# A hybrid decoder block with 64 experts: gate and up weights issued ahead of the preceding expert's down weights

## The reference

```python
t = h.reshape(B * S, D)
scores = jax.nn.sigmoid((t @ w_router).astype(jnp.float32))
...
w = w / jnp.sum(w, axis=-1, keepdims=True) * ROUTED_SCALE
combine = (jax.nn.one_hot(eidx, N_EXPERTS, dtype=jnp.float32) * w[..., None]).sum(1).astype(t.dtype)
y = (jax.nn.silu(t @ w_sh_gate) * (t @ w_sh_up)) @ w_sh_down
for g in range(N_GROUPS):
    sl = slice(g * EXPERTS_PER_GROUP, (g + 1) * EXPERTS_PER_GROUP)
    a = jax.nn.silu(jnp.einsum('td,edf->tef', t, w_gate[sl])) * jnp.einsum('td,edf->tef', t, w_up[sl])
    y = y + jnp.einsum('tef,efd->td', a * combine[:, sl, None], w_down[sl])
```

## Time and profile before

| | us |
|---|---|
| median of 3 runs | 1158.05 (1157.08 to 1160.28) |
| span of the profiled execution | 1155.5 |
| TensorE busy in it | 1109.0 |
| VectorE, ScalarE, GpSimd busy | 854.7, 783.1, 413.2 |
| q1 (SyncE's queue): moved, share of the 16 engines' time | 254.13 MB, 56.6% |

### The profile page before, as it was taken

The page is one execution under the profiler, slowest core; times in us unless marked ns, Lnnn a source line. Parts: engine busy times, 40 slices in busy tenths (PEclk is TensorE's granted clock), DMA queues, the critical chain, the costliest instruction groups (busy, mean ns, idle before and its releaser), DMA issues. The chain is left out here.

```text
span 1155.5 us, 17715 instructions
## 1 busy us (share of the span) xinstructions
PE 1109.0 (96%) x5459; PEld 909.9 (79%) x5459; DVE 854.7 (74%) x1211; ACT 783.1 (68%) x1266; POOL 413.2 (36%) x477
## 2 busy tenths in 40 slices
PE   7999999999899999999999999999999999999898
PEld 7888888788678886888888887777878878777677
DVE  3536534277664586999999988888899989899665
ACT  6644434367553335888888888788888888887562
POOL 1220000033473002455555553444555555454320
PEclk9999999999999999999999999999999999999999
DMA  6422322113203098999999999999999999999631
GB/s 241 146 73 82 136 73 75 38 60 101 100 2 128 37 367 311 379 322 358 383 388 385 384 386 377 362 359 361 369 362 371 366 365 379 366 369 364 173 123 73
DMA packets 71955, 291.61 MB, mean 252 GB/s; under 512 B 15139, under 2 KB 20550, under 8 KB 46950
## 3 DMA queue, kind: packets, MB, share of 16 engines
q1 hardware_dynamic: 52496, 254.13, 56.6%
q0 software_dynamic: 18768, 34.79, 11.9%
q10 hardware_dynamic: 646, 2.12, 0.5%
HBM read 284.61 MB, written 42.07 MB: 283 GB/s over the span
## 5 line engine op out<-in xcount | busy, mean ns | idle before, releaser
L1518 DVE TENSOR_TENSOR arena_r<-arena,win_r 128x1024 fp32r<-128x1024 f32 x252 | 292.1, 1220 | 51.7 <-ACT win_r L986 46.7
L986 ACT ACTIVATE win_r<-arena 128x1024 fp32r<-128x1024 f32 x252 | 246.2, 1056 | 57.8 <-DMA arena<-in_w_exp_up 53.4
L1929 PE MATMUL bank<-win_r,work_r 128*128 128x512 f32 x512 | 205.3, 401 | 19.6 <-DVE x_low_r L1477 19.1
L669 POOL DMA_INDIRECT moe_sum<-ya,sidx x64 | 121.0, 1890 | 252.4 <-ACT ya L1019 252.4
L1930 PE MATMUL bank<-win_r,x_low_r 128*128 128x512 f32 x512 | 199.4, 390 | 0.0
L1931 PE MATMUL bank<-arena_r,work_r 128*128 128x512 f32 x504 | 197.0, 391 | 0.0
L1492 DVE TENSOR_TENSOR arena_r<-arena,hT_r 128x1024 fp32r<-128x1024 f32 x128 | 150.5, 1218 | 0.0
L1929 PEld LDWEIGHTS bank<-win_r,work_r 128*128 128x128 f32 x512 | 96.3, 188 | 43.8 <-issue 25.9
L1663 PE MATMUL bank<-arena_r,hT_r 128*128 128x512 f32 (+2 forms) x320 | 121.8, 381 | 1.2 <-DVE win_r L1129 1.2
L1667 PE MATMUL bank<-win_r,hT_r 128*128 128x512 f32 (+2 forms) x320 | 120.4, 376 | 0.0
L1664 PE MATMUL bank<-arena_r 128*128 128x512 f32 (+2 forms) x320 | 120.4, 376 | 0.0
(11 more groups left out here) (290 smaller groups left out, 2173.3 us busy)
## 6 DMA issues: line engine op xcount, KB each, us to landing
arena<-in_w_exp_down SPq DMA_DIRECT2D x64, 1024.0 KB, 15.8
arena<-in_w_exp_gate SPq DMA_DIRECT2D x63, 1024.0 KB
arena<-in_w_exp_up SPq DMA_DIRECT2D x63, 1024.0 KB
win<-in_w_in SPq DMA_DIRECT2D x8, 2048.0 KB, 7.7
win<-in_w_o SPq DMA_DIRECT2D x2, 2048.0 KB, 7.9
arena<-in_w_ple_gate SPq DMA_DIRECT2D x2, 2048.0 KB, 24.5
arena<-moe_sum SPq DMA_DIRECT2D x8, 512.0 KB, 7.6
win<-in_mla_w_qb SPq DMA_DIRECT2D x4, 576.0 KB, 4.0
```

Source lines behind the costliest of these rows:

```text
L669: pool.indirect_dma_start(sums[j % 2], bass.IndirectOffsetOnAxis(sidx[j % 2][0:NS, 0:1], 0), yo[j % 2][0:NS], None, bounds_check=last_toke ...
L986: act.activation(gu_hi[n % 2][:, :, cols], raw[:, :, cols], ACT.Copy).then_inc(gu_hi_r, 1)
L1518: dve.tensor_tensor(low_[:, :, cols], raw[:, :, cols], gu_hi[n % 2][:, :, cols].bitcast(F32), ALU.subtract).then_inc(gu_lo_r, 1)
L1929: pe.matmul(b_, x_hi[:, k, :], w_hi, start=(k == 0), stop=False)
```

## The change

SyncE's order of issue. Gate and up of expert e are issued as soon as the slot's gate and up part is free, and the down weights of expert e-1 after them, where before down of e-1 came first. The condition for each transfer is the same as before. The last expert's down weights follow by themselves after the loop. Ahead of the loop, gate and up of expert 8 are issued before down of expert 3 and before the last of the four blocks of the shared result; a wait for expert 4's gate and up to have landed is added there, since both count on the same semaphore.

```diff
             expert_gu(3, 3)
-            for t, (y_, n) in enumerate(((sh_y_act, 1), (sh_y_dve, 1), (sh_y_dve, 2), (sh_y_act, 2))):
-                if t == NT - 1:
-                    sp.wait_ge(sh_dn, NT)
-                    expert_dn(3, 3)
+            def shared_rows(t, y_, n):
                 sp.wait_ge(y_, n)
                 sp.dma_start(sums[1][t * P:(t + 1) * P, :], y_sh[t]).then_inc(sum_odd_st[t // 2], 16)
 
-            for e in range(RING, 3 * RING):
-                sp.wait_ge(gu_done, e - RING + 1)
+            for t, (y_, n) in enumerate(((sh_y_act, 1), (sh_y_dve, 1), (sh_y_dve, 2))):
+                shared_rows(t, y_, n)
+            sp.wait_ge(gu_done, 1)
+            sp.wait_ge(w_gu[0], 64)
+            expert_gu(2 * RING, 0)
+            sp.wait_ge(sh_dn, NT)
+            expert_dn(RING - 1, RING - 1)
+            shared_rows(NT - 1, sh_y_act, 2)
+
+            for e in range(RING + 1, 3 * RING):
                 if e != 2 * RING:
-                    expert_gu(2 * RING if e == EXTRA else e, e % RING)
-                sp.wait_ge(dn_done, e - RING + 1)
-                expert_dn(e, e % RING)
+                    sp.wait_ge(gu_done, e - RING + 1)
+                    expert_gu(e, e % RING)
+                sp.wait_ge(dn_done, e - RING)
+                expert_dn(e - 1, (e - 1) % RING)
             with sp.Fori(3, E // RING) as q:
                 for r in range(RING):
                     sp.wait_ge(gu_done, q * RING + (r - RING + 1))
                     expert_gu(q * RING + r, r, one=False)
-                    sp.wait_ge(dn_done, q * RING + (r - RING + 1))
-                    expert_dn(q * RING + r, r, one=False)
+                    sp.wait_ge(dn_done, q * RING + (r - RING))
+                    expert_dn(q * RING + (r - 1), (r - 1) % RING, one=False)
+            sp.wait_ge(dn_done, E - RING)
+            expert_dn(E - 1, RING - 1)
             sp.wait_ge(nb_ready, 1)
```

More of the change, by code:

```diff
@@ L487, in _ @@
                         expert_gu(e, e % RING)
-                        sp.wait_ge(dn_done, b * E + (e - RING + 1))
-                        expert_dn(e, e % RING)
+                        if e >= 1:
+                            sp.wait_ge(dn_done, b * E + (e - RING))
+                            expert_dn(e - 1, (e - 1) % RING)
                     with sp.Fori(2, E // RING) as q:
@@ L493, in _ @@
                             expert_gu(q * RING + r, r, one=False)
-                            sp.wait_ge(dn_done, b * E + q * RING + (r - RING + 1))
-                            expert_dn(q * RING + r, r, one=False)
+                            sp.wait_ge(dn_done, b * E + q * RING + (r - RING))
+                            expert_dn(q * RING + (r - 1), (r - 1) % RING, one=False)
+                    sp.wait_ge(dn_done, b * E + (E - RING))
+                    expert_dn(E - 1, RING - 1)
             sp.dma_start(pbuf, a["p"][0, 0].rearrange("(t q) n -> q t n", q=P)).then_inc(ld_p, 16)
```

## The result

The changed kernel takes 1164.1 us (median of 12 runs, 1157.4 to 1173.4) against 1158.74 for the kernel before; ratio 1.0056, 95% interval 1.0036 to 1.0076. A second series gives 1168.48 and 1.0099 (1.0079 to 1.0119); the two intervals do not touch, so a single series says less about this kernel than its interval suggests. The forecast was 1153.2, range 1148 to 1158. Not only is the time longer, it is also less steady: the kernel before spreads over 7 us, this one over 16.

A forecast was written before the change was run, and what follows sets the result against it. TensorE was taken to bound the loop's first part (9.47 us a step), weights the second (10.10). Terms 3.4 + 1.6 - 0.2 = 4.8 us off the 1155.5 span gave 1150.7, plus 2.55 made 1153.2; range 1148 to 1158.

The forecast's parts named there:

- The order's term: SP's queue: gate/up has one 1 MB transfer less ahead of it and lands earlier; 3.4 us, bounds 0 and 3.8.
- ScalarE's cover for the down weights: Down lands 3.4 us late behind gate/up, but ScalarE needs it 3.8 us after; cover 0.4 us thin.
- The moment's term: Gate/up issued 4.3 us sooner in step 5 gains only where the queue stands empty: 1.6 us, bounds 0 and 4.3.
- fills what was idle: From 507.1 to 511 us the earlier issue uses idle DMA share, so every later expert's weights land 1.6 us earlier.
- the hole of 507 to 511 us: Last place where the weight queue stands empty, DMA share 0.60; priced at 4 x (1 - 0.60) = 1.6 us.
- Expert 8 ahead of the shared rows: Before the loop, 2 MB go ahead of down(3) and the last shared row block: cost 0 to 1 us once, 0.2 taken.
- rival 4: Slower: gathers share engines with weights, steps 8 to 30; decisive beyond 0.22 us a step later; 1163, chance 0.10.
- Its sign: Waits for gathered rows at L1895 before 671 us, 4.5 us in all, grow by more than 5 us.
- From span to time: Median of runs taken as 2.55 us above the profiled span: 1150.7 becomes 1153.2.
- the prediction's reading of the page: All DMAs interleave on the same 16 engines, so only the hole would count, not the order: 1156.6.

## Why the prediction was wrong

**What bounded the kernel** was read rightly: weights in the second part, at the pace of 10.1 us. Two runs bear it out: with gathers early and the old order nothing changes (1157.5), and with both, where the weights have their lead and no gather is late, it gets faster (1147.7).

**The order's term**, 3.4 us, measured 2 us (0.9981 of the time, interval 0.6 to 3.8 us) where gathers are still tight, and 3.7 to 4.7 where they are not. Both agree with 3.4 within what these runs can tell. ScalarE's cover for the down weights held: no wait for down in any list.

**The moment's term** was mis-sized: 1.6, measured 5.3 to 6.8 where no gather is late. The step that failed is that the new order "fills what was idle", priced as the hole of 507 to 511 us, 4 x (1 - 0.60). The hole was 2.8 us and not 1.6, since 503 to 507 us had a share of 0.71, and it was not filled: 2.6 us of it are left, now mostly from 499 to 503 us, and the gain came all the same. Nor was the issue 4.3 us earlier there: gate of expert 9 went out at 506.78, 2.7 us earlier, as the loop itself was 2 us late. So the idle share of the engines does not price the lead. A likely reason, not shown, is that the queue is not backed up in the early steps (a down transfer landed 5.0 us after its issue), so that a transfer issued sooner lands sooner by all of that. The bound given, 4.3 us, lies within what the runs can tell; what the rest is, stays open.

**Expert 8 ahead of the shared rows**: 0.2 taken, 0 to 1 bounded. The write behind the block was 2.1 us later, beyond the bound. With the whole step alone the time is unchanged (0.9996), in a kernel whose end the weights set; in the changed kernel, where they do not, up to 2 us of the loss may be this.

**What was missing from the sum**, and turned a gain into a loss, is the gather. It stood in the prediction as rival 4, with 0.10, with its place (L1895, steps in which TensorE sets the pace) and its threshold (a gather later by more than 0.22 us a step). Its sign came true: the weight load's waits for rows from 470 to 671 us grew from 4.5 to 11.0, more than the 5 named.

```profile
PEld bank L1906 <- DMA ya<-h_rows,gidx: 11.0, 12, 1.6
```

The rows for more were at hand: gathers were already waited for in the part where TensorE sets the pace, which says that their slack there is nil. The step of the prediction that failed is that it looked only at SP's own queue for what the earlier burst moves past, and so put the gathers' cost at nothing in the sum. GpSimd's queue shares the engines, and the gather's moment, 6.1 us behind one burst and 3.3 ahead of the next, should have been set beside the new moment of the burst. The sum then is: gain of the lead, up to 10 us, against a pace of (10.6 + landing)/2 in place of 9.47, which at 9.1 us of landing is 9.85 in the first part, and the same in the second, where it beats the weights' 10.10 by little. The profiled execution shows 9.91 and 9.82, a draw. Its runs without a profile are 3 to 16 us longer; that they lose most of it to the gathers is supported by the three kernels that changed only the gather's time (1147.7 and 1149.7 with it sooner, 1188.5 with it later), but it was not seen in a profile, and a part is the clock's.

**From span to time** the prediction added 2.55 us, which compares one execution's span with the median of others. For one and the same execution the runs show 1.8 us (1157.4 and 1155.6). This is small beside the miss.

**The Trainium skill weighed against the trace**: by the prediction's reading of the page "DMA: Bandwidth & Descriptors", section "Issuing engines are not separate DMA queues", the order would be worth nothing and the sum 1156.6. The runs give the order 3.7 to 4.7 us. The page's sentence is about starting transfers from several engines at once; here all of them stay on one queue and only their order changes, and the prediction stretched the sentence over that.

## What to carry to other kernels

When a burst of transfers is moved in time, look up what every other queue issues at the new moment, and how many microseconds that has in hand. A small indirect gather on a path that closes over two steps can cost more than the burst gains. A resource that is waited for a little in the part where another engine sets the pace has no slack: give it room first (here: issue the gather before waiting for the scatter's result) and then make the change, which together gave 0.9912 where the change alone gave 1.0056 and the room alone 0.9999.

## What the runs showed of the hardware

- A gather of 128 rows (of 1088 float32, 557 KB) took 8.0 to 9.9 us from issue to landing beside full weight traffic. Issued with 2 MB entering 0.8 us ahead of it, it was waited for in 44 of some 60 steps; with 1 MB in 20, where the kernel before has 15.
- A kernel whose pace hangs on such gathers is less steady: 16 us of spread in the changed kernel and 13 in the one with the gather delayed, against 2 to 7 us in the others. Twice the profiled execution was its kernel's shortest (1157.4 and 1157.2). The mean granted clock falls in these kernels too, to 0.995 in the longest run of the first and 0.991 in a run of 1192.7 us of the second. That TensorE's more frequent stops bring the clock down, and what the rest of the spread is, was not tried.
- At a DMA share of 1.00 the weights arrived at 10.0 to 10.1 us for each expert, whatever was issued sooner (10.10 before, 10.01 with gather first, over the steps in which they were waited for). Why no faster stays open. The Trainium skill, page "DMA: Bandwidth & Descriptors", section "Latency and other measured facts", says that two of the sixteen DMA engines are usually slower than the others; no row here separates them.
